# Feeding the high and low input parts of the down projections to TensorE in one 512-column matmul

## The reference

```
def conv_ffn(h, w_gu, conv_w, conv_b, w_down):
    a, u = jnp.split(h @ w_gu, 2, axis=-1)
    a = causal_depthwise_conv(a, conv_w, conv_b)
    return (jax.nn.silu(a) * u) @ w_down
...
        h = rms_norm(x, norm_ffn[i])
        x = x + conv_ffn(h, ffn_w_gu[i], ffn_conv_w[i], ffn_conv_b[i], ffn_w_down[i])
```

## Time and profile before

| what | value |
|---|---|
| median of three runs | 1120.69 us (1118.94 to 1124.15) |
| the profiled execution: its span, the only time that its page gives | 1119.2 us |
| TensorE, matmuls | 1095.6 us, 98% of the span, 9175 instructions |
| TensorE, weight loads | 1048.5 us, 94% |
| VectorE / ScalarE / GpSimd | 65% / 51% / 40% |
| granted TensorE clock | 1.00 in the windows of both down projections (2.4 GHz) |
| down projection, layer 0 | 290.8 to about 354.7 us |
| down projection, layer 1 | about 562 to 626 us |

### The profile page before, as it was taken

How to read it: one execution, slowest core, us unless ns; L and a number is a source line. 1 busy time by engine, 2 the same in 40 slices (tenths; PEclk the granted TensorE clock), 3 DMA queues, 4 the chain that set the end, 5 groups by cost and what they waited for, 6 DMA issues and landing times.

```text
span 1119.2 us, 23474 instructions
## 1 busy us (share of the span) xinstructions
PE 1095.6 (98%) x9175; PEld 1048.5 (94%) x9175; DVE 731.5 (65%) x1029; ACT 574.7 (51%) x827; POOL 449.2 (40%) x430
## 2 busy tenths in 40 slices
PE   7999999999999999999999999999999999999998
PEld 6897799999999869999999999999998989999997
DVE  6776757777555866877746564558747668777543
ACT  5546755544443665555535447645346445544333
POOL 4464714666402661666622112213533014666300
PEclk9999999999999999999999999999999999999999
DMA  9740147766555416666645454243334445766552
GB/s 286 248 129 23 40 133 209 196 184 184 187 170 170 151 43 185 186 189 186 186 163 181 156 184 150 79 151 114 115 112 151 151 114 158 200 181 182 188 181 76
DMA packets 226408, 175.40 MB, mean 157 GB/s; under 512 B 8720, under 2 KB 207632, under 8 KB 226208
## 3 DMA queue, kind: packets, MB, share of 16 engines
q1 hardware_dynamic: 225056, 173.00, 51.3%
q10 hardware_dynamic: 1248, 1.35, 0.4%
q0 software_dynamic: 32, 0.03, 0.0%
HBM read 173.32 MB, written 1.05 MB: 156 GB/s over the span
## 4 chain that ended last, share of the span: by engine, by line
PE 83%; DVE 5%; ACT 4%; POOL 3%; issue 3%; DMA 2%; SPq 0%; DVEq 0%; POOLq 0%; ACTq 0%
PE psum L630 24%; PE psum L636 23%; PE psum L631 23%; PE psum L696 2%; ACT w_h L1423 2%; DVE w_l L1882 1%; PE psum L833 1%; DMA raw<-in_nsa_w_in 1%; PE psum L1268 1%; POOL work L2767 1%; POOL work L2769 1%; PE psum L1100 1%; PE psum L860 1%; PE psum L1355 1%; PE psum L806 1%
## 5 line engine op out<-in xcount | busy, mean ns | idle before, releaser
L630 PE MATMUL psum<-xh,w_h 128*128 128x256 f32 (+3 forms) x1760 | 438.4, 286 | 9.9 <-ACT w_h L1488 7.4
L631 PE MATMUL psum<-xl,w_h 128*128 128x256 f32 (+3 forms) x1760 | 432.3, 283 | 0.0
L630 PEld LDWEIGHTS psum<-xh,w_h 128*128 128x128 f32 (+1 forms) x1760 | 331.6, 188 | 15.3 <-ACT w_h L1488 7.4
L631 PEld LDWEIGHTS psum<-xl,w_h 128*128 128x128 f32 (+1 forms) x1760 | 332.4, 189 | 0.5
L1882 DVE TENSOR_TENSOR w_l<-raw,w_h 128x2048 fp32r<-128x2048 f32 (+2 forms) x91 | 202.7, 2228 | 140.8 <-ACT w_h L1423 140.8
L1423 ACT ACTIVATE w_h<-raw 128x2048 fp32r<-128x2048 f32 x92 | 167.8, 1824 | 202.3 <-PE psum L636 184.4
L636 PE MATMUL psum<-xh,w_l 128*128 128x256 f32 (+3 forms) x1760 | 245.7, 282 | 0.7 <-DVE w_l L1882 0.7
L636 PEld LDWEIGHTS psum<-xh,w_l 128*128 128x128 f32 (+1 forms) x1760 | 224.6, 188 | 1.9 <-DVE w_l L1882 1.2
L2664 POOL TENSOR_TENSOR work<-work 128x256 f32<-128x256 f32 x66 | 160.7, 2434 | 135.5 <-ACT work L1621 135.5
L2201 DVE TENSOR_TENSOR w_l<-raw,w_h 128x2048 fp32r<-128x2048 f32 x66 | 151.4, 2293 | 13.9 <-ACT w_h L1608 13.3
L630 PE MATMUL psum<-hid_h,w_h 128*128 128x256 f32 (+1 forms) x592 | 148.4, 282 | 0.5 <-issue 0.5
(11 more groups left out here) (329 smaller groups left out, 1414.5 us busy)
## 6 DMA issues: line engine op xcount, KB each, us to landing
raw<-in_ffn_w_gu SPq DMA_DIRECT2D x88, 512.0 KB, 5.0
raw<-in_w_in SPq DMA_DIRECT2D x26, 1024.0 KB, 5.0
raw<-in_ffn_w_down SPq DMA_DIRECT2D x40, 512.0 KB, 4.6
raw<-in_w_ffn_up SPq DMA_DIRECT2D x22, 512.0 KB, 3.9
raw<-in_w_ffn_gate SPq DMA_DIRECT2D x22, 512.0 KB, 5.2
raw<-in_w_ffn_down SPq DMA_DIRECT2D x20, 512.0 KB, 4.3
raw<-in_nsa_w_in SPq DMA_DIRECT2D x9, 1024.0 KB, 6.2
raw<-in_swa_w_qkv SPq DMA_DIRECT2D x5, 1024.0 KB, 5.3
```

The source lines that it names most:

```text
L630: mm(dst, parts[0][:, k, cols], high, start=first, stop=False)
L631: mm(dst, parts[0][:, k, cols], low, start=False, stop=False)
```

## The change

`hid_h` and `hid_l` become two slices of one buffer. In layers 0 and 1 the down projection's high terms become one matmul for each k: its moving operand is `hid_pair[:, :, k, :]`, two runs of 256 columns (the high part and the low part of block k), and its output is the whole bank of 512 columns. The low-weight terms still add into the first half. On DVE, `put` adds both halves of the bank to `xT`, the second after the first has finished. Layer 2 keeps its form.

```
-        hid_h = nc.alloc_sbuf_tensor_at("hid_h", [128, FC, T2], F32R, offset=big_at)
-        hid_l = nc.alloc_sbuf_tensor_at("hid_l", [128, FC, T2], F32R, offset=big_at + 4 * FC * T2)
+        hid_hl = nc.alloc_sbuf_tensor_at("hid_hl", [128, 2, FC, T2], F32R, offset=big_at)
+        hid_h, hid_l = hid_hl[:, 0, :, :], hid_hl[:, 1, :, :]
...
+                hid_pair = hid_hl[:, :, :, :].rearrange("p s f t -> p s (f t)")[:, :, 0:FC * T].rearrange("p s (f t) -> p s f t", t=T)
+
+                def two_halves(dst):
+
+                    return dst.rearrange("p (s t) -> p s t", s=2)
+
...
-                                dst, cols = bank[down_bank(44 + 4 * g + c)][:, 0:T], slice(128 * c, 128 * c + 128)
+                                dst, cols = bank[down_bank(44 + 4 * g + c)][:, 0:T if l == 2 else 2 * T], slice(128 * c, 128 * c + 128)
                                 for k in range(k0, k1):
-                                    high_terms(dst, parts, k - k0, cols, hh[:, k, :], hl[:, k, :], k == 0)
+                                    if l == 2:
+                                        high_terms(dst, parts, k - k0, cols, hh[:, k, :], hl[:, k, :], k == 0)
+                                    else:
+                                        mm(two_halves(dst), parts[0][:, k - k0, cols], hid_pair[:, :, k, :], start=k == 0, stop=False)
...
                 def put(c):
-                    add_chunk(N_FFN[l] + 44, c)
+                    n = N_FFN[l] + 44 + c
+                    dve.wait_ge(proj_done, n + 1)
+                    line.put(V.tensor_tensor(xT[:, c, 0:T1], bank[bank_of(n)][:, 0:T1], xT[:, c, 0:T1], ALU.add))
+                    line.settle()
+                    line.put(V.tensor_tensor(xT[:, c, 0:T1], bank[bank_of(n)][:, T1:2 * T1], xT[:, c, 0:T1], ALU.add), proj_taken)
```

## The result

The changed kernel took 1125.49 us (median of 6 runs, 1124.04 to 1127.06) against 1120.87 us for the kernel before: a ratio of 1.0043, 95% interval 1.0029 to 1.0057, that is 3.2 to 6.4 us slower. The forecast was 1124.6 us. The profiled executions have spans of 1123.6 and 1119.2 us.

The account below looks back on a forecast made before the run. TensorE's stream, busy 98%, was taken as the bound. Losses of 0.9 + 1.5 + 1.05 + 1.46 = 4.9 us less 1.0 us gave +3.9, 1124.6 us; range 1118.0 to 1128.5, the forecast's own range 1122.5 to 1126.5.

Parts of the forecast that it names:

- a pair saves: Down projections, layers 0 and 1: one 512-column matmul takes 233.5 ns where two of 256 took 237, saving 3.5 ns.
- 296 pairs that count: Down projections: 148 of 176 pairs a layer shorten the time, the others precede waits on DVE; gain 1.0 us.
- fourth chunk, layers 0 and 1: Hand-over between groups: PE waits 1.05 us for DVE's adds, restart adds some 0.1; 1.15 us.
- layer 0, wait of 0.24 us for a slab goes: PE's wait at 334.92 for a slab's low part vanishes, since that slab comes by DMA; net 0.9 us.
- layer 1, slab late after the adds: DVE's slab of 602.57 ends at 607.2 to 607.6, PE wants it at 607.0; 0.4 us more loss.
- next stage, layer 0: Hand-over after the last part: later puts delay POOL's last square and the last `xl`; PE 1.05 us later.
- next stage, layer 1: Hand-over after the last part: PE already waits for `xl` and takes the whole delay of 1.46 us.
- clock after that wait: Behind PE's wait for `xl` after layer 1: the prediction gave no loss from a falling clock.
- rival A: Wide matmuls: the column costs 0.417 ns, the rest is fixed; a pair saves 12 ns, 1122.0 us; chance 0.19.
- rival B: Wide matmuls: a pair saves 22 ns, as the plain float32 rows have it, 1119.1 us; chance 0.14.
- Rival C: Wide matmuls: the two-run operand costs a restart of 6 to 10 ns at its second run, 1127.4 us; chance 0.13.

Follow-up runs that it names:

- the first four experiments: Four variants of the changed kernel: one add, split matmuls, second half taken early, inputs side by side; the kernel before took 1120.49 us beside them.
- e4_early: Against the changed kernel: part 5 goes narrow into the first half, DVE adds the second half earlier while idle; 1119.41 us, ratio 0.9992.

## Why the prediction was right

The total came out 0.9 us from the forecast, in its own range, and on the side forecast. The mechanism was the one described: no gain from the columns, a small one from the matmuls saved, and two hand-overs at which TensorE waits for DVE. Its terms, with what the traces show:

| step | forecast | shown |
|---|---|---|
| a pair saves | 3.5 ns | 6.7 ns |
| 296 pairs that count | -1.0 us | -2.0 us |
| fourth chunk, layers 0 and 1 | +1.15 each | +1.1 each |
| layer 0, wait of 0.24 us for a slab goes | -0.24 | -0.24 |
| layer 1, slab late after the adds | +0.4 | +1.3 |
| next stage, layer 0 | +1.05 | +1.3 |
| next stage, layer 1 | +1.46 | +1.4 |
| clock after that wait | none | +1.5 |
| sum | +3.9 | +5.5 |

The places are read as distances from the chain's start. ACT's half slab starts at 350.24 and PE's second half at 358.52, 8.28 us, against 6.98 us in the kernel before (351.84 and 358.82); in layer 1 it is 8.21 (624.71 to 632.92) against 6.83 us (623.20 to 630.03). The fourth chunk starts 5.51 us after DVE's slab (319.68 and 325.19) against 4.43. In layer 1 the low matmuls that need the late slab start 15.40 us after DVE's slab (592.21 and 607.61) against 12.98 (592.95 and 605.93), of which 1.1 is the fourth chunk's wait. These are the starts of the chain, first in the kernel before, then in the changed one, there with POOL's last square of layer 0:

```profile
351.84 2.01 ACT L1432 ACTIVATE w_h<-raw 128x1024 fp32r<-128x1024 f32 x2 [4.64 <-PE psum L636]
623.20 2.01 ACT L1432 ACTIVATE w_h<-raw 128x1024 fp32r<-128x1024 f32 x2 [4.64 <-PE psum L636]
```

```profile
350.24 2.01 ACT L1441 ACTIVATE w_h<-raw 128x1024 fp32r<-128x1024 f32 x2 [4.54 <-PE psum L636]
624.71 2.01 ACT L1441 ACTIVATE w_h<-raw 128x1024 fp32r<-128x1024 f32 x2 [4.54 <-PE psum L636]
...
356.59 1.52 POOL L2702 TENSOR_TENSOR sq<-xT 128x256 f32<-128x256 f32 x1 [0.40 <-DVE xT L2285]
```

The sum is checked by two landmarks that both kernels have, ACT's slabs before and after the changed stretches: the one at 222.85 comes at 221.52, 1.33 us early, the one at 637.08 at 641.48, 4.40 us late. Between them lie 5.7 us, of which the table has 5.5. In the kernel before and in the changed one the landmarks are

```profile
222.85 1.92 ACT L1608 ACTIVATE w_h<-raw 128x2048 fp32r<-128x2048 f32 x1 [0.24 <-PE psum L636]
637.08 1.91 ACT L1423 ACTIVATE w_h<-raw 128x2048 fp32r<-128x2048 f32 x1
```

```profile
221.52 1.92 ACT L1617 ACTIVATE w_h<-raw 128x2048 fp32r<-128x2048 f32 x1
641.48 1.91 ACT L1432 ACTIVATE w_h<-raw 128x2048 fp32r<-128x2048 f32 x1
```

That the profiled spans differ by only 4.4 us is the 1.33 us from ahead of all changed code: there the profile of the kernel before has a stretch at the 1.2 GHz level (granted clock 0.50 from 72 to 75 us) that the other has not. ACT's slab before it starts 0.31 us earlier than in the changed kernel (65.08 and 65.39), the one behind it 1.25 us later (76.91 and 75.66). So part of the closeness is luck: the gain of the pairs was put too small by 1.0 us, and 2.6 us of loss were missed.

Four terms were mis-sized. **The pair**: 3.5 ns rested on 0.45 ns a column, and 512 columns cost 232.5 ns, within 1 ns of the 233.5; that was right, and the fixed cost of 11.6 ns (rival A, 225 ns) and the price of the plain float32 rows (rival B, 215 ns) are excluded. The rest of the 6.7 ns is the narrow matmul: inside the down projection it had cost 118.9 ns and not 118.3, and the four low ones, too, run 1.4 ns faster now. That the text took 237 ns for a pair where the earlier trace rows give 238 was a slip of 1 ns. The formula of the Trainium skill (TensorE: Matmul & The Clock Gate, Back-to-back issue gap) gives an estimate of 216 ns. The measurement decides: 232.5 ns, so the formula does not hold for this type here. Rival C is excluded: the two runs cost nothing. **The next stage in layer 0**: the fourth put ends 6.27 us after the start of ACT's half slab in place of 4.81, late by the forecast 1.46, but POOL's last square, which starts while DVE makes its half slab, takes 1.52 us and not the 0.92 of the text. **The slab in layer 1**: I added the delay and 0.4 us, on the thought that `xl` might run beside POOL; what really ran into POOL's sums were the three small operations before it, which tripled. **The clock**: that a wait of 2.2 us lets the clock fall was not weighed at all, though the text had the wait.

Three readings of the text were wrong, and none of them moved the sum by more than 0.3 us. The 215 ns of the earlier trace rows are not the distance of a plain float32 matmul: the profile shows each of these matmuls as two rows (16 rows of line 730 for the 8 matmuls that `sum_rest` issues in the two layers), so one of 256 columns costs 430 ns, and rival B took the price of half a matmul. In layer 0 POOL did not end a wait of PE: the list of waits of the kernel before has none there, and with 0.43 us a sum the last one is due at 358.57, 0.2 us after POOL's last square. And the 0.47 us of the matmul at 358.82, taken as what a break after a wait costs, has no wait in its row; that matmul follows the plain float32 ones.

## What to carry to other kernels

Fewer and wider matmuls of the same columns give back only what a matmul costs beside its columns, here 5 to 7 ns each; read that from two widths in the same trace before paying for it elsewhere. Ask what a second half of an accumulator costs at the moment when somebody waits for it: the same adds, done one part earlier in the engine's idle time, brought no wait. A step that is delayed can land beside another engine's work and take three times as long, so look at what it is moved next to. And where a change adds a wait of TensorE, read the granted clock behind it: here 2.2 us of waiting were followed by 1.5 us more.

## What the runs showed of the hardware

- 512 columns of fp32r in two runs cost 232.5 ns at the full clock, 0.454 ns a column, 9% over one column a cycle at 2.4 GHz; in one run they cost 1 or 2 ns more.
- A plain float32 matmul of 256 columns shows as two rows, 215 ns each and 430 ns together (633.56 to 633.99 in the earlier trace rows), where one of fp32r costs 118 ns.
- Two adds of DVE from PSUM start 0.33 us apart where the second does not need the first, and 0.46 us apart where it does.
- The run to run scatter of one kernel goes with the mean granted clock of the run. The runs of the kernel before beside the first four experiments, sorted by it: 0.999, 9 runs, median 1118.8 us; 0.997, 6 runs, 1120.6 us; 0.996, 4 runs, 1122.2 us; 0.995, 3 runs, 1121.8 us. The mean clock in turn goes with the number of stretches at the 1.2 GHz level: among the profiled executions of the experiments the one without any has 0.999, those with one 0.996 or 0.997, with two 0.996, with three 0.994. The profiled execution of e4_early has three such stretches inside its work, at 72, 396 and 748 us, and took 1120.8 us; its run at 0.999 took 1117.4 us. At equal clock e4_early was 1.3 to 1.8 us faster than the kernel before (0.999, 0.997 and 0.996). But four of its twelve runs were at 0.994, where the kernel before has none, and whether the early adds bring such stretches is open.

```profile
72.00:75.00 3.00, 3.00 (x16) 3.00 (x16) 2.65 (x5) 0.00 (x0) 2.71 (x4) 0.51 0.59 208
396.50:399.50 3.00, 3.00 (x17) 1.56 (x14) 0.35 (x2) 0.80 (x4) 2.71 (x3) 0.50 0.00 0
748.00:751.00 3.00, 3.00 (x16) 3.00 (x15) 2.96 (x7) 0.00 (x0) 0.00 (x0) 0.50 0.31 67
```

These are windows of that execution, the eighth column of numbers being the granted clock. Which execution meets which of these stretches was not under control in any run.
